# One 512-column matmul for high and low tokens, two results filled into PSUM, two weight sums by adding DMAs, in the gate/up stage of a transformer layer

## The reference

```python
D_MODEL = 2048; SEQ = 512
D_FF = -(-8 * D_MODEL // (3 * 256)) * 256        # 5632

def _swiglu(h, w_gate_up, w_down):
    gu = h @ w_gate_up                            # 512 x 2048 @ 2048 x 11264
    g, u = gu[..., :D_FF], gu[..., D_FF:]
    return (jax.nn.silu(g) * u) @ w_down
```

## Time and profile before

| | |
|---|---|
| time, median of 3 runs | 1776.34 us (1774.98 to 1778.63) |
| time of the profiled execution | 1774.28 us |
| its span, first to last instruction | 1772.3 us |
| PE busy | 1744.5 us, 98% |
| DVE, ACT, POOL busy | 1261.8, 725.8, 102.1 us |
| units by `unit`, from about 505 to 1332 us | 41 |
| matmuls of 512 columns, 24 of plain work | 5.44 us |
| matmuls of 256 columns, 24 (one part) | 2.88 us |

### The profile page before, as it was taken

The page is one execution under the profiler, slowest core; times in us unless marked ns, Lnnn a source line. Parts: engine busy times, 40 slices in busy tenths (PEclk is TensorE's granted clock), DMA queues, the critical chain, the costliest instruction groups (busy, mean ns, idle before and its releaser), DMA issues.

```text
span 1772.3 us, 28857 instructions
## 1 busy us (share of the span) xinstructions
PE 1744.5 (98%) x11224; PEld 1589.9 (90%) x11224; DVE 1261.8 (71%) x1285; ACT 725.8 (41%) x862; POOL 102.1 (6%) x130
## 2 busy tenths in 40 slices
PE   8999999999999999999999999999999999999997
PEld 6888888888899999999999999999997788888885
DVE  6432433335888877888778877788789888888886
ACT  5232322235444444444444444444445344434454
POOL 3000000003000000000000000000001000000044
PEclk9999999999999999999999999999999999999999
DMA  8333232252234444334443344433449885876854
GB/s 238 79 88 92 74 95 71 72 213 76 68 120 120 142 149 136 118 118 138 134 130 118 118 138 150 138 119 118 139 148 283 245 244 165 228 214 203 249 130 131
DMA packets 294751, 254.73 MB, mean 144 GB/s; under 512 B 8112, under 2 KB 257200, under 8 KB 288432
## 3 DMA queue, kind: packets, MB, share of 16 engines
q1 hardware_dynamic: 288848, 224.71, 40.7%
q0 software_dynamic: 3456, 23.07, 6.6%
q10 hardware_dynamic: 2400, 6.29, 0.9%
HBM read 203.72 MB, written 27.26 MB: 130 GB/s over the span
## 4 chain that ended last, share of the span: by engine, by line
PE 93%; DVE 3%; issue 1%; DMA 1%; ACT 1%; POOL 1%; SPq 0%; ACTq 0%; POOLq 0%; DVEq 0%
PE ps L1920 31%; PE ps L1704 22%; PE ps L1981 21%; PE ps L1927 16%; PE ps L1902 2%; PE ps L1907 1%; DVE tmp L1235 1%; DMA operand_raw<-a_sums 1%; DVE hT_lo L1223 0%; DVE xres L1563 0%; PE ps L1717 0%; POOL xres L801 0%; DVE split_lo L1539 0%; DMA xres<-in_x_dram 0%; DVE split_lo L1216 0%
## 5 line engine op out<-in xcount | busy, mean ns | idle before, releaser
L1013 ACT ACTIVATE split_hi<-raw 128x1024 fp32r<-128x1024 f32 x295 | 312.1, 1058 | 462.4 <-DVE raw L1426 398.3
L1415 DVE TENSOR_TENSOR split_lo<-raw,split_hi 128x1024 fp32r<-128x1024 f32 x295 | 358.5, 1221 | 115.6 <-ACT split_hi L1013 108.6
L1981 PE MATMUL ps<-split_hi,operand_hi 128*128 128x512 f32 x616 | 240.7, 391 | 6.1 <-DVE xres L1563 4.2
L1920 PE MATMUL ps<-hT_lo,split_hi 128*128 128x256 f32 x984 | 241.4, 283 | 0.0
L1920 PE MATMUL ps<-hT_hi,split_hi 128*128 128x256 f32 x984 | 241.4, 283 | 0.0
L1981 PE MATMUL ps<-split_hi,operand_lo 128*128 128x512 f32 x616 | 239.8, 389 | 0.0
L1086 ACT ACTIVATE split_hi<-down_slot 128x2048 fp32r<-128x2048 f32 (+1 forms) x84 | 148.3, 1773 | 214.1 <-DVE down_slot L1548 105.6
L1426 DVE TENSOR_TENSOR raw<-raw 128x1024 f32<-128x1024 f32 x164 | 200.3, 1221 | 7.7
L1920 PEld LDWEIGHTS ps<-hT_lo,split_hi 128*128 128x128 f32 x984 | 188.9, 192 | 0.0
L1920 PEld LDWEIGHTS ps<-hT_hi,split_hi 128*128 128x128 f32 x984 | 188.9, 192 | 0.0
L1539 DVE TENSOR_TENSOR split_lo<-down_slot,split_hi 128x2048 fp32r<-128x2048 f32 (+1 forms) x84 | 177.1, 2109 | 14.4 <-ACT split_hi L1086 14.4
(11 more groups left out here) (181 smaller groups left out, 2990.9 us busy)
## 6 DMA issues: line engine op xcount, KB each, us to landing
raw<-in_ffn_w_gate_up_dram SPq DMA_DIRECT2D x172, 512.0 KB, 4.3
down_slot<-in_ffn_w_down_dram SPq DMA_DIRECT2D x40, 1024.0 KB, 7.1
raw<-in_fox_w_in_dram SPq DMA_DIRECT2D x24, 1024.0 KB, 5.8
a_sums<-pack SPq DMA_DIRECT2D x22, 1024.0 KB, 6.3
down_slot<-down_slot POOLq DMA_DIRECT2D x20, 1024.0 KB, 7.3
operand_raw<-a_sums SPq DMA_DIRECT2D x35, 512.0 KB, 5.1
raw<-in_fox_w_out_dram SPq DMA_DIRECT2D x8, 1024.0 KB, 5.0
xres<-in_x_dram SPq DMA_DIRECT2D x4, 1024.0 KB, 8.6
```

What stands on the lines that cost most here:

```text
L1013: nc.scalar.activation(ring(r, 0, n), source, ACT.Copy).then_inc(t_hi, 1)
L1415: nc.vector.tensor_tensor(ring(r, 1, n), source, f32(ring(r, 0, n)), ALU.subtract).then_inc(t_lo, 1)
L1920: ins = nc.tensor.matmul(out, ring(at.r, 0, n)[:, k * P:(k + 1) * P], tokens[part][:, k * HALF:(k + 1) * HALF], start=bool(fresh) and k == ...
L1981: ins = nc.tensor.matmul(banks[:, tile, :], operand[e][part][:, i, tile * P:(tile + 1) * P], down_ring(dn, part_of_t, e)[:, i * BANK:(i + ...
```

## The change

Four things change in `unit`, on all engines.

1. The high and low parts of every token operand now lie in one tensor (`hT`, `oT`, `s3`, `split` get a dimension of two), and one matmul of 512 columns multiplies a tile of high weights with both: the left 256 columns of a bank take the high tokens' product, the right 256 the low tokens'. The low weights still go with high tokens alone, into the left half. All parts take whole banks, and two sets of four banks serve units in turn.
2. The left and right halves have to be added afterwards: ACT takes the left half (`take_left`), DVE adds the right one (`add_right`), three times per unit. Silu of both gate halves is one instruction of 512 columns.
3. Product 0 is copied by ACT from its bank into bank 3 of the set (`copy_first`, PSUM to PSUM), and the difference that up's first half needs is written by DVE into bank 2; parts 3 and 5 then accumulate onto them. The order of parts 3 to 5 changes (SEVEN).
4. B12+B22 and B11+B21 are no longer DVE additions but adding DMAs that POOL issues, each with a small GpSimd instruction ahead. SP's loads are issued in another order.

```diff
-        SEVEN = ((A11, 0), (S1, 1), (S2, 0), (S4, 2), (S3, 0), (A12, 3), (A22, 0))
+        SEVEN = ((A11, 0), (S1, 1), (S2, 0), (A12, 3), (S3, 0), (S4, 2), (A22, 0))
+        PART_OF = ("B11", "B11", "B11", "B21", "B12", "B22", "B11")
+        UNIT_BANKS = ((0, 1, 2, 3), (4, 7, 5, 6))
...
+            def part_by_dma(at, j, into, other, done):
+                if at.r is not None or j:
+                    pool.wait_ge(part_turns, counted(2, 8, at.r, 2 * at.nth + j))
+                x1, x2 = (slot(place(at.r, name, at.u)[0]) for name in (into, other))
+                nc.gpsimd.tensor_tensor(out=turn_of[:], in0=half[:], in1=half[:], op=ALU.add).then_inc(part_turns, 1)
+                pool.dma_start(x1, x2, accum_op=ALU.add).then_inc(done, 16)
+            def unit_sums(at):
+                pool.wait_ge(t_sum, at.sums(1))
+                wait_loaded(pool, at.r, "B22", at.u)
+                part_by_dma(at, 0, "B12", "B22", added3)
+                pool.wait_ge(t_lo, at.part(2))
+                wait_loaded(pool, at.r, "B21", at.u)
+                part_by_dma(at, 1, "B11", "B21", added4)
```

ScalarE's `unit` (`gate_before` is `take_left` of the last unit's gate and then Silu of 512 columns):

```diff
             def unit(at):
                 if at.r is not None:
-                    gate_two_before(at)
+                    gate_before(at)
                 sum_hi(at, 2)
-                copy_q(at, 0)
+                copy_first(at)
-                plain_hi(at.r, at.first + 3, "B22", at.u)
-                copy_q(at, 1)
+                plain_hi(at.r, at.first + 3, "B21", at.u)
+                copy_second(at)
                 sum_hi(at, 4)
-                plain_hi(at.r, at.first + 5, "B21", at.u)
+                plain_hi(at.r, at.first + 5, "B22", at.u)
+                act.wait_ge(product, at.product(3))
+                act.wait_ge(a_done, at.acts())
+                take_left(ga[:, 0:HALF], bank_of(at, 3))
                 sum_hi(at, 6)
                 if not end:
                     plain_hi(at.r, at.first + 7, "B11", at.u + 1)
-                gate_one(at)
-                if not end:
+                act.wait_ge(product, at.product(5))
+                take_left(cc[:, 0:HALF], bank_of(at, 2))
+                if end:
+                    down_hi(Down(None, 0), 0)
+                    split_operand(Down(None, 0), 0)
+                else:
                     sum_hi(at.next(), 1)
```

VectorE's `unit`:

```diff
             def unit(at):
                 unit_lo(at, 1)
+                if at.r is not None:
+                    gate_right_before(at)
                 second_sum(at)
                 if at.r is not None:
                     act_before(at)
                 unit_lo(at, 2)
                 unit_lo(at, 3)
-                dve.wait_ge(t_sum, at.sums(2))
-                sum_of(at, "B12", "B22")
...
+                combine(bank(at, 2), qq[:], bank(at, 0), ALU.subtract)
+                unit_lo(at, 4)
+                unit_lo(at, 5)
+                dve.wait_ge(x_taken, at.taken(1))
+                add_right(ga[:, 0:HALF], bank_of(at, 3))
+                dve.wait_ge(product, at.product(4))
+                combine(qq[:], qq[:], bank(at, 0), ALU.subtract)
+                unit_lo(at, 6)
+                combine(cc[:, HALF:S], qq[:, 0:HALF], qq[:, HALF:S], ALU.add)
+                if not end:
+                    unit_lo(at.next(), 0)
+                dve.wait_ge(x_taken, at.taken(2))
+                add_right(cc[:, 0:HALF], bank_of(at, 2))
```

TensorE, one part and the unit's waits:

```diff
             def half_product(at, e):
                 for k in range(QK8):
-                    for part in range(2):
-                        ins = nc.tensor.matmul(out, ring(at.r, 0, n)[:, k * P:(k + 1) * P],
-                                               tokens[part][:, k * HALF:(k + 1) * HALF],
+                    ins = nc.tensor.matmul(both, ring(at.r, 0, n)[:, k * P:(k + 1) * P],
+                                           tokens[2][:, :, k * HALF:(k + 1) * HALF],
+                                           start=e < 2 and k == 0, stop=False, skip_group_check=True)
...
             def unit(at):
-                    pe.wait_ge(q_copied, at.copied(0))
+                    pe.wait_ge(combined, at.combined(-5))
                 half_product(at, 0)
-                    pe.wait_ge(combined, at.combined(-2))
                 half_product(at, 1)
                 pe.wait_ge(q_copied, at.copied(1))
                 half_product(at, 2)
-                    pe.wait_ge(combined, at.combined(0))
                 half_product(at, 3)
                 pe.wait_ge(combined, at.combined(1))
                 half_product(at, 4)
-                    pe.wait_ge(silu_done, at.silu(0))
                 half_product(at, 5)
                 pe.wait_ge(combined, at.combined(3))
                 half_product(at, 6)
```

More of the change, by code:

```diff
@@ L600, in load_after @@
                 more = G - at.u - 1 if is_last(at.r) else 2
-                if more:
-                    sp.wait_ge(t_sum, at.sums(3))
-                    load_part(at.r, "B22", at.u + 1)
+                if more > 1:
+                    sp.wait_ge(t_lo, at.part(4))
+                    load_part(at.r, "B12", at.u + 2)
                 if at.r is None:
@@ L1063, in unit @@
                     split_operand(Down(None, 0), 0)
-                sum_hi(at, 6)
-                if not end:
-                    plain_hi(at.r, at.first + 7, "B11", at.u + 1)
-                gate_one(at)
-                if not end:
+                else:
                     sum_hi(at.next(), 1)
@@ L1420, in unit_lo @@
             def unit_lo(at, e):
-                named_lo(at.r, at.first + e, ("B11", "B11", "B11", "B22", "B12", "B21", "B11")[e], at.u)
+                named_lo(at.r, at.first + e, PART_OF[e], at.u)
             def sum_of(at, into, other):
@@ L1440, in bank, with combine, add_right, gate_right_before @@
             def bank(at, which):
-                return ps[:, bank_of(at, which), 0:HALF]
+                return ps[:, bank_of(at, which), :]
+            def combine(out, in0, in1, op):
+                nc.vector.tensor_tensor(out, in0, in1, op).then_inc(combined, 1)
+            def add_right(out, bank):
+                combine(out, out, ps[:, bank, HALF:S], ALU.add)
+            def gate_right_before(at):
+                dve.wait_ge(x_taken, at.taken(0))
+                add_right(ga[:, HALF:S], bank_before(at))
             def plain_out(f, into):
@@ L1926, in half_product @@
                 for k in range(QK8):
-                    ins = nc.tensor.matmul(out, ring(at.r, 1, n)[:, k * P:(k + 1) * P],
+                    ins = nc.tensor.matmul(both[:, 0, :], ring(at.r, 1, n)[:, k * P:(k + 1) * P],
                                            tokens[0][:, k * HALF:(k + 1) * HALF],
```

156 lines of the change are left out of this document (81 added, 75 removed).

## The result

The changed kernel takes 1778.84 us (median, 1775.13 to 1781.67), the kernel before 1776.34 (1774.0 to 1778.69): ratio 1.0015, 95% interval 1.0008 to 1.0021. That is no gain, and by its interval a small loss, where 1763.5 was forecast. The profiled execution took 1775.13 us (before: 1774.28).

What follows compares the result with a forecast made beforehand. The prediction took PE, without gaps, to bound the units. From the profiled 1774.28 us it took 30.6, added 15.2 for waits and 2.8 for down's start, giving 1761.7; with the median's 2.06 it forecast 1763.5, range 1750 to 1780.

Steps and rivals of the forecast that it cites:

- 0.25 to 0.55: Main forecast: PE waits this many us ahead of part 2 of each unit, time 1758 to 1771; chance 0.62.
- 30.6 to be won: In the units, 287 parts each 0.107 us shorter by 8 fewer matmuls, if PE stays without gaps.
- 15.2 to be given back: At the seam of units, PE waits 0.38 us ahead of part 2 for ACT's copy, in 40 units.
- 0.7 for the late start of the down product: Down's first high part waits for product 5, not 3, so down's part 0 starts 0.7 us late.
- The part, 2.773: On TensorE, 8 matmuls of 512 columns (1.813) and 8 of 256 (0.960) take 2.773 us, 0.107 less than before.
- it doesn't do what it says: Rival: fixed 13.3 ns per matmul not saved; parts 2.86 or so, chain about 0.1 late, near 1775; chance 0.05.
- PE at +8.70: At the seam, PE starts part 2 about 8.70 us after part 6's start, behind the copy ending at +8.64.
- The wait costs only itself: After the wait ahead of part 2, four parts follow in 11.09 us, giving a unit of 19.79.
- its half of the gain hangs on fixed steps: The wait at the seam cannot shrink, so a unit saves 0.37 us, half of 0.75.
- The adding DMAs, hidden: In the units, the second adding DMA takes about 6 us of 7.75 allowed, so it costs 0.
- The end of the stage, 2.8: At the start of down, its part 2 comes at +13.7 instead of +10.93, costing 2.8 us.
- both a little worse: The case of no measurable change in time, which the prediction gave a chance of 0.08.

Runs made afterwards that it cites:

- experiment 5: Changed kernel with the low weights too through one 512-column matmul, a different computation that only measures a part's length: 1996.06 us.
- experiment 3: Changed kernel with B12+B22 and B11+B21 added by DVE again, no adding DMAs in the units: 1778.0 us, ratio 1.0015.
- the fill: Changed kernel with 3, 6 and 7 unread 512-column matmuls in PE's waits at the start of the down product: 1776.86 us, ratio 1.0004.
- experiment 7: Unread matmuls in PE's waits at the down product's start: 1776.86 us in the changed kernel, 1756.51 us with the copy of product 0 also ahead of hi 2.
- experiment 4: Changed kernel with two matmuls of 256 columns for the one of 512: 1790.78 us, ratio 1.0087.
- experiment 8: Changed kernel with product 0's copy ahead of hi 2, unread matmuls at the down product's start, and 6 and 8 more in later waits: 1755.61 us, ratio 0.9884.
- experiment 6: Changed kernel with DVE's add of the left half of cc moved behind sum 1, in all units but the last: 1771.71 us, ratio 0.9972.
- experiment 1: Changed kernel with ACT's copy of product 0 ahead of hi 2 instead of behind it: 1760.54 us, ratio 0.9911.
- experiment 9: Changed kernel with ACT's copy of product 0 ahead of hi 2 and DVE's add of cc's left half behind sum 1: 1757.57 us, ratio 0.9895.
- experiment 2: Changed kernel with ACT's copy of product 0 one place later, behind hi 3: 1813.84 us.

## Why the prediction was wrong

Its mechanism was right: one wait per unit, ahead of part 2, released by the copy, and 0.44 us long on average, inside its 0.25 to 0.55. Its sign was wrong. In the stretch of the units it had 30.6 to be won, 15.2 to be given back and 0.7 for the late start of the down product, so 14.7 left; the profile shows 826.55 - 824.09 = 2.5. Three steps failed, all in the same direction.

- **The part, 2.773.** It is 2.793. The step "24 of 512 columns take 5.44, 0.2267 each", taken over to a stream that alternates, failed by 0.020 a part: 287 x 0.020 = 5.7 us of the 30.6 (experiment 5). I had this as the rival "it doesn't do what it says" and gave 0.05 to its full size, a fifth of which came. Per merged pair the part saves (2.88 - 2.793) / 8 = 10.9 ns. The Trainium skill (TensorE: Matmul & The Clock Gate, Back-to-back issue gap) would have it 2.5 ns; the trace is far nearer to 13.3.
- **PE at +8.70.** It came at +8.83. Both steps from a sum to its high took 1.38 for the 1.34 that I carried over (hi 1 0.04 late, hi 2 0.08); PE starts 0.13 behind the copy's end, where I allowed 0.06 and no row of the kernel before showed a PE that waits for this copy. The copy itself was right (0.58 for 0.60). Parts 0.020 longer hide 0.06 of the 0.13, so the waits come to 17.4 us for 15.2.
- **The wait costs only itself.** No term stood for what follows it: part 2 is 2.89 long, 0.10 more than others, 4.0 us in 40 units. This term, put at nothing, is the largest miss after the part. With 5.7 and 2.2 it makes 11.9 of the 12.2 that are missing. The prediction had noted that its half of the gain hangs on fixed steps; it didn't draw the consequence, that with TensorE at 2.793 and the chain at 8.83 a unit saves 0.06, and an error of 0.1 in the chain costs 4 us.
- **The adding DMAs, hidden.** Right in the loop (4.7 us to landing, experiment 3). Once, in the last unit, hi 6 stood 3.89 us for its adding DMA; the unit is 0.27 longer than with the sums on DVE. The rest of its 20.73 us is the wait of 0.78 ahead of the down product, 0.65 with the sums on DVE.
- **The end of the stage, 2.8.** Right: down's part 0 starts 0.78 late, and its part 2 at 1339.74, 13.71 behind T6 (1326.03), as forecast. What was not seen is that its idle places may draw the clock down in some runs; the kernel before had only two of them, of 0.36 and 1.77 us:

```profile
1333.38 0.47 PE L2044 MATMUL ps<-split,operand_hi 128*128 128x512 f32 x1 [0.75 <-ACT split L1151]
1336.78 1.21 PE L2044 MATMUL ps<-split,operand_hi 128*128 128x512 f32 x4 [1.35 <-DVE split L1613]
1339.74 0.47 PE L2044 MATMUL ps<-split,operand_hi 128*128 128x512 f32 x1 [1.75 <-DVE xres L1637]
```

  The changed kernel's median lies 3.7 above its profile, in which no clock fell at this place, that of before 2.1 above its own, which the forecast added. That is 1.6 us more; with the fill the median is 2.0 lower, so the fill may account for it, but experiment 7 leaves that open. Part of the spread is older: in every kernel the stretch before the units takes 504.2 to 507.4, by the clock of the first 50 us.

The sum as it came: 1774.28 - 24.9 (287 x 0.087) + 17.4 (the waits) + 4.0 (the slow starts of part 2) + 0.9 (the last unit's 0.78 and 0.13) + 2.1 (down product) + 1.1 is 1774.9, against 1775.13. The last 1.1 lies behind PE's last matmul. The last store is issued 8.9 behind that matmul in both kernels and lands 3.0 later before, 4.1 later in the changed one. It isn't the change's: in experiments 4 and 8, with the same code at the end, the tail is as short as before (12.4 us, 13.4 in the others).

What the chances missed: I took the row-by-row chain for good to 0.1 us in 20. A forecast that rests on the small difference of two terms of 30 and 15 should have had the case "both a little worse" at more than 0.08. It was also mispriced: for parts of 2.86 and a chain 0.1 late, said to give about 1775, the prediction's own sum gives 8.80 + 4 x 2.86 = 20.24 a unit, and with 2.8 and 2.06 some 1782, a loss. (Its main sum comes to 1763.7, not 1763.5.)

## What to carry to other kernels

When an engine is made faster, the unit's new length is not its busy time but the longest chain across engines; write the chain's links from the timeline, and ask of each instruction on it whether it must stand there. Here one copy of 0.58 us that nothing just ahead of it fed stood behind a 1.06 us conversion that waited, and moving it up one line was worth 18 us (1778.84 to 1760.54), more than the merging by itself (12, from 1790.78 to 1778.84). Price also what comes right after a wait, and look whether the chain is longer inside a hardware loop than outside. An engine that gets idle places may also lose its clock: look for matmuls at twice their distance behind the waits, in more than one profile, and try a fill if the waits can't be closed.

## What the hardware showed that I had not expected

- Eight matmuls of 512 columns behind 256-column ones take 1.84 us, behind 512-column ones 1.813; so 27 ns at that change of shape. Eight of 256 behind 512-column ones take 0.953 us, 7 ns less than 8 x 0.120, hence 0.020 a part.
- After a wait of 0.45 us TensorE's first 512-column matmul is followed 0.33 us later, not 0.227, at full granted clock.
- The hand-overs of the chain are longer inside the hardware loop than behind it: DVE's sum to ACT's high 1.38 and 1.25 us, the end of ACT's copy to PE's matmul 0.13 and 0.05.
- A DVE instruction of 1024 columns is followed 1.14 later by one that doesn't wait for it, and 1.24 to 1.35 later by one that waits for its end because it writes over what the first reads (1.24 and 1.35 in the earlier trace rows, 1.26 and 1.35 in experiment 6).
- A copy of 128 x 512 from PSUM to PSUM on ACT takes 0.58 us, no more than with one end there.
- The granted clock fell by half behind waits of 0.8, 1.3 and 1.8 us, for some 5 us, in the profiles of experiments 1, 4, 5 and 9 and not in those of the changed kernel and experiments 2, 3 and 6, which have the same waits. What decides it was not found.
